# State-space decay without the causal mask product: Relu per head, one Exp over eight heads

## The reference, cut to what matters

```python
a_cs = jnp.cumsum(dt * A, axis=2)                      # A = -exp(a_log), so a_cs falls along time
seg = a_cs[:, :, :, None] - a_cs[:, :, None, :]        # a_l - a_s
decay = jnp.exp(jnp.where(causal, seg, -jnp.inf))      # 0 where s > l
cb = jnp.einsum('bclgn,bcsgn->bclsg', Cc, Bc)
y_diag = jnp.einsum('bclsg,bclsgr,bcsgrp->bclgrp', cb, decay, x)
states = ...                                           # carried from chunk to chunk
y = (y_diag + y_off) + d_skip * xh
```

## Time and profile before

| what | value |
|---|---|
| median of 3 runs | 1325.18 us (1324.61 to 1326.75) |
| span of the profiled execution, first to last instruction | 1311.2 us |
| median less span | 14.0 us |
| PE busy | 1269.9 us, 97% of the span |
| DVE busy | 640.5 us, 49% |
| ACT busy | 384.1 us, 29% |
| POOL busy | 725.5 us, 55% |
| mean granted PE clock | 0.996 |

### The profile page before, as it was taken

The page is one execution under the profiler, slowest core; times in us unless marked ns, Lnnn a source line. Parts: engine busy times, 40 slices in busy tenths (PEclk is TensorE's granted clock), DMA queues, the critical chain, the costliest instruction groups (busy, mean ns, idle before and its releaser), DMA issues.

```text
span 1311.2 us, 19028 instructions
## 1 busy us (share of the span) xinstructions
PE 1269.9 (97%) x7452; PEld 919.5 (70%) x7452; DVE 640.5 (49%) x1030; ACT 384.1 (29%) x763; POOL 725.5 (55%) x750
## 2 busy tenths in 40 slices
PE   8999989999999999999999999999999899999997
PEld 7888768787788776888888887788878333333333
DVE  4252361448993584624865678843315432222225
ACT  5211272422332584112122654441004011111111
POOL 6677636576675401766774445666771565555430
PEclk9999999999999999999999999999999999999999
DMA  6623311433232200343321314632277599999965
GB/s 232 188 75 107 96 34 31 151 121 97 65 129 97 97 1 1 96 133 120 102 64 52 94 49 145 266 135 97 95 287 292 215 373 408 406 403 405 402 244 192
DMA packets 86557, 216.40 MB, mean 165 GB/s; under 512 B 24260, under 2 KB 33196, under 8 KB 72900
## 3 DMA queue, kind: packets, MB, share of 16 engines
q1 hardware_dynamic: 62844, 199.23, 41.3%
q0 software_dynamic: 14064, 8.45, 2.2%
q10 hardware_dynamic: 9560, 7.51, 1.8%
HBM read 252.85 MB, written 25.96 MB: 213 GB/s over the span
## 4 chain that ended last, share of the span: by engine, by line
PE 74%; DMA 10%; DVE 7%; ACT 3%; DVEq 2%; POOL 2%; issue 1%; SPq 1%; ACTq 0%; POOLq 0%
PE ps L184 18%; PE ps L185 17%; PE ps L186 17%; DMA w_gu<-w_up 9%; PE ps L1204 7%; PE ps L1219 3%; PE ps L872 2%; POOL w_lo L1283 1%; PE ps L993 1%; PE ps L1077 1%; PE ps L1001 1%; DVE pr L2166 1%; ACT pr L1465 1%; SPq L559 1%; PE ps L971 1%
## 5 line engine op out<-in xcount | busy, mean ns | idle before, releaser
L1280 POOL CAST w_hi<-stage 128x512 fp32r<-128x512 f32 (+1 forms) x280 | 176.8, 674 | 358.6 <-PE ps L186 348.8
L1283 POOL TENSOR_TENSOR w_lo<-stage,w_hi 128x512 fp32r<-128x512 f32 (+1 forms) x280 | 367.7, 1345 | 10.1
L184 PE MATMUL ps<-hi,w_hi 128*128 128x512 f32 (+1 forms) x608 | 236.8, 389 | 0.8 <-ACTq L1666 0.5
L186 PE MATMUL ps<-lo,w_hi 128*128 128x512 f32 (+1 forms) x608 | 235.0, 386 | 0.0
L185 PE MATMUL ps<-hi,w_lo 128*128 128x512 f32 (+1 forms) x608 | 235.0, 386 | 0.0
L184 PE MATMUL ps<-w_hi,hi 128*128 128x512 f32 (+1 forms) x488 | 176.1, 361 | 2.4 <-DVE xtok L2290 0.9
L186 PE MATMUL ps<-w_lo,hi 128*128 128x512 f32 (+1 forms) x488 | 174.7, 358 | 0.0
L185 PE MATMUL ps<-w_hi,lo 128*128 128x512 f32 (+1 forms) x488 | 174.7, 358 | 0.0
L1204 PE MATMUL ps<-w_gu,xT 128*64 128x512 f32 x736 | 164.7, 600 | 3.7 <-DMA w_gu<-w_up 3.3
L184 PEld LDWEIGHTS ps<-hi,w_hi 128*128 128x128 f32 x608 | 114.2, 188 | 27.4 <-issue 3.4
L186 PEld LDWEIGHTS ps<-lo,w_hi 128*128 128x128 f32 x608 | 114.2, 188 | 23.3
(11 more groups left out here) (487 smaller groups left out, 1787.6 us busy)
## 6 DMA issues: line engine op xcount, KB each, us to landing
stage<-w_in SPq DMA_DIRECT2D x84, 512.0 KB, 4.5
w_gu<-w_gate SPq DMA_DIRECT2D x32, 1024.0 KB, 13.4
w_gu<-w_up SPq DMA_DIRECT2D x32, 1024.0 KB, 16.0
w_dn<-w_down SPq DMA_DIRECT2D x32, 1024.0 KB, 11.9
stage<-w_out SPq DMA_DIRECT2D x16, 512.0 KB, 4.6
stage<-w_ssd_branch SPq DMA_DIRECT2D x16, 512.0 KB, 4.7
stage<-w_in SPq DMA_DIRECT2D x20, 256.0 KB, 3.1
stage<-w_attn_branch SPq DMA_DIRECT2D x8, 512.0 KB, 4.3
```

The source lines that it names most:

```text
L184: pe.matmul(out, x[0], w[0], start=first, stop=False)
L186: return pe.matmul(out, x[0], w[1], start=False, stop=last)
L1280: nc.gpsimd.tensor_copy(hi[:, b, k, 0:n], stage[:, b, k, 0:n])
L1283: last = nc.gpsimd.tensor_tensor(lo[:, b, k, 0:n], stage[:, b, k, 0:n], hi[:, b, k, 0:n].bitcast(F32), ALU.subtract)
```

## The change

The mask product on PE (L1055) goes away, with the two DVE instructions that made `mask_r` and `ident_r`. ACT computes `relu(a_s - a_l)` for each head from PSUM, and then one Exp with scale -1 over eight heads, in place in SBUF. Where s > l the Relu gives 0 and the Exp 1; the zero comes from `cb`, which already carries the triangle. `acs[:, 0]` now holds `a_s` itself and not its negative. PE waits for `m_ready` once for each eight heads, and not once for the chunk. The waits for the four banks in `spread` stay, but no matmul stands between them now.

```diff
             def spread(c, half):
                 s = turns.take(ALL)
                 for b in range(4):
                     turns.bank(b, turns.k)
-                    pe.matmul(ps[s][:, b, :].rearrange("p (h l) -> p h l", h=4), ident_r[:], bc(mask_r[:], 1, 4), start=True, stop=False)
                 for j in range(4):
                     for b in range(4):
...
-                                         acs_rows[rows, P * c:P * (c + 1)], start=False, stop=(j == 3))
+                                         acs_rows[rows, P * c:P * (c + 1)], start=True, stop=True)
...
             pe.wait_ge(acs_copied, 1)
-            pe.wait_ge(acs_ready, 1)
...
-                pe.wait_ge(m_ready, 4 * (c + 1))
                 pe.wait_ge(xd_ready, c + 1)
                 s = turns.take()
                 for h in range(32):
+                    if h % 8 == 0:
+                        pe.wait_ge(m_ready, 4 * c + h // 8 + 1)
...
-            A.activation(acs[:, 2], acs[:, 0], ACT.Exp, scale=-1.0)
+            A.activation(acs[:, 2], acs[:, 0], ACT.Exp)
...
-                        last = A.activation(decay[:, hh, :], ps[s][:, h // 4, P * (h % 4):P * (h % 4 + 1)], ACT.Exp,
-                                            bias=acs[:, 0, c, hh:hh + 1])
+                        last = A.activation(decay[:, hh, :], ps[s][:, h // 4, P * (h % 4):P * (h % 4 + 1)], ACT.Relu,
+                                            scale=-1.0, bias=acs[:, 0, c, hh:hh + 1])
                         if h % 8 == 7:
-                            last.then_inc(e_ready, 1)
                             A.drain().then_inc(turn_free[s], 1)
+                            some = decay[:, hh - 7:hh + 1, :]
+                            A.activation(some, some, ACT.Exp, scale=-1.0).then_inc(e_ready, 1)
...
-            V.tensor_scalar(acs[:, 0], sums[:, :, 0, :], -1.0, None, ALU.mult)
+            V.tensor_copy(acs[:, 0], sums[:, :, 0, :])
...
-            V.tensor_tensor(acs[:, 1], acs[:, 3], acs[:, 0], ALU.add)
-            V.wait_ge(mT_saved, 16)
-            V.tensor_scalar(mask_r[:], tri[:], -1.0, -NEG, ALU.add, ALU.mult)
-            V.tensor_copy(ident_r[:], ident[:])
+            V.tensor_tensor(acs[:, 1], acs[:, 3], acs[:, 0], ALU.subtract)
             V.drain().then_inc(acs_ready, 1)
```

More of the change, by code:

```diff
@@ L322, in program @@
         acs = at("acs", 116, [P, 4, TT, 32])
-        mask_r, ident_r = at("mask_r", 112, [P, P], F32R), at("ident_r", 112.5, [P, P], F32R)
         sgb = at("sgb", 72, [P, KC, S])
```

## The result

The kernel after takes 1334.74 us (median of 4 runs, 1333.57 to 1337.79), the kernel before on the same chip 1325.14 us. The ratio is 1.0076, with a 95% interval of 1.0064 to 1.0088. It is slower by 9.6 us (difference of the medians) or 10 us (by the ratio), where 7.8 were forecast. A later comparison (e10) gave 1.0077 (1.0063 to 1.0092).

The account below looks back on a forecast made before the run. The prediction took ACT followed by DVE to bound the SSD stage, not PE; longer ACT groups and unhidden table loads, less the mask's saving, delay the last z projection 7.8 us: 1325.2 + 7.8 = 1333.0 us, range 1327.5 to 1337.

Parts of the forecast that it names:

- S0 to S3: Starts of ACT's first decay activation in chunks 0 to 3 of the SSD stage; forecast 724.4, 749.6, 778.6, 809.5.
- Groups of eight: ACT's eight Relus plus one Exp: 3.25 us a group, DVE's last multiply at S + 13.1, or S + 14.5 in chunks 1 to 3.
- The table load: Exp's load falls unhidden between first eight Relus and first Exp in chunks 1 to 3, 1.4 us each; rival, stays hidden: chance 0.13.
- Its 2.66 us for a switch: The skill's price for a table switch, load plus drain; by it the forecast would be 3.8 us higher.
- My sum: Chunk-by-chunk sum of ACT and DVE times to the last z projection: 837.8 against 829.95, 7.8 us later.
- The delay passes on: After the last z projection no slack absorbs the delay, so all 7.8 us reach the end; no-change rival: chance 0.05.

Follow-up runs that it names:

- e10: The kernel after, unchanged, measured again on another chip; ratio to the kernel before 1.0077.
- e3: Kernel after plus a one-column Exp behind the Silu of chunks 0 to 2, loading the table in ACT's idle time; ratio to before 1.0045.
- e2: Kernel after with one Exp per head (scale 0, timing only) in place of Relu and Exp over eight heads, still without mask matmuls; ratio to before 0.9999.
- e5: Kernel after with DVE's skip term moved ahead of the first multiply and from_state ahead of the second; ratio to before 1.0006.
- e4: Kernel after with the mask matmuls back in spread, Relu and Exp over eight heads kept; ratio to before 1.0105.
- e6: Kernel after with DVE's skip term and from_state moved, the early table load, and chunk 3's unread xe left out; ratio to before 1.0000.
- e8: e6 with mask matmuls back in the second spread of every chunk, as filler; ratio to before 0.9994.
- e9: e8 with the filler mask matmuls in the second spread of chunks 1 to 3 only; ratio to before 0.9995.
- e1: The kernel before, unchanged, measured and profiled again; ratio to before 0.9995.

## Why the prediction came out as it did

The direction, the mechanism and most of the size were right. Point by point, in distances from the stage's first table load, since everything before it ran 0.6 us earlier in this profile:

- **S0 to S3.** Forecast 2.0, 27.2, 56.2 and 87.1 us after the load (724.4 to 809.5 less 722.43). Measured 1.9, 26.8, 56.1 and 87.9 (723.77, 748.61, 777.96 and 809.71 less 721.86).
- **Groups of eight.** Forecast 3.25 us apart, measured 3.23; last multiply at S + 13.1 in chunk 0 and S + 14.5 later, measured 13.06 and 14.4.
- **The table load.** It fell where forecast, 2.27 us after S1. It cost 1.28, and 1.30 to the next activation; the runs with and without it (after and e3) differ by 3.6 us of D and 4.1 us of time, near my 4.1. From the end of the last Relu to the start of the Exp it is 1.39 us in chunk 1, drain and load together, where I had taken 1.4. The Trainium skill's place for the load was right (ScalarE: Activation LUTs, section Table sets). Its 2.66 us for a switch (section What ACT_TABLE_LOAD costs) did not show. The time alone could not have told: 1334.7 lies between my 1333.0 and the 1336.8 by its figure. (Its surplus over my 1.4 is 1.26 us a switch and not 1.28; the 3.8 us for three stand.)
- **The parts add up in D.** Mask gone 2.4 us less (e2), Exps over eight heads 7.2 more (e3 less e2), table loads 3.6 more (after less e3): 8.4 in all, which is 115.9 - 107.5. My sum gave 7.8.
- **The cause is ACT's time in series with DVE's.** The same ACT work costs little once DVE does the skip term and from_state before its multiplies: 1.9 us of D (e5 less e2), and nothing against before in the time (1.0006, interval over 1).
- **The delay passes on.** From D to E it grew by 1.3 us more (131.5 us after, 130.2 before), and E came 9.7 us later, which is the 10 us of the ratio.

The term that was mis-sized is the last: I passed on 7.8 us and reckoned with PE at full clock behind the new waits. PE waited 3.9 us, then ran at half clock, 8 matmuls where 14 fit, and lost 1.3 us there that nothing hid. The other profiles bear this out. The four with half clock at the start of the last z projection (after, e3, e10, e4) need 131.5, 131.7, 131.9 and 132.3 us from D to E; the eight without need 130.2 to 130.5. The half-clock stretches in chunks 1 and 3 cost the kernel after nothing that I can find, since DVE was the later one there.

The rest of the miss, 0.6 us of D, is a balance. S0 came 0.1 us early, chunk 0 was 0.35 us shorter than in my sum, chunk 1 0.35 longer and chunk 2 0.85 longer (31.75 us from S2 to S3 and not 30.9), the end 0.2 shorter. In chunk 2, L2286 began 8.9 us after the last multiply and S3 came 8.5 us after that, where I had 8.5 and 7.9. That the total came so close owes something to these terms of both signs.

I had also read the 14.0 us between span and median as if it lay around the span. It did not matter, because only a difference was added to the median, but comparing the two spans would have given twice the true effect.

Not tried: two or three Exps a chunk of other sizes, and another order of spreads and tokens on PE that would fill the wait before the second spread with useful work.

## What to carry to other kernels

Work moved from the busiest engine to an idle one is free only if nothing waits in line behind it: ask what follows the idle engine's last instruction, and add both. Here ACT was idle for 70% of the span, yet each group's extra microsecond came straight through because DVE had up to 6 us of unrelated work queued behind its last multiply; moving that work ahead of the wait gave back 9 us. Splitting a function in two can also bring a table load out of idle time, and a one-column activation of the right kind puts it back.

## What the runs showed of the hardware that was not expected

- The granted clock of PE fell to half, 1.2 GHz, after waits of a few microseconds in the stage: once behind the bank waits of chunk 3 in e2, twice in e6, three times in the kernel after.
- It does not follow from the length of the wait. In the kernel after PE waited 2.8 us before the second spread of chunk 2 and the clock stayed up; in e10, the same kernel, it fell behind the same 2.8 us. It also fell in e10 in chunk 0 (from about 722.5 us on) behind a wait of 1.4 us, where in the first profile it stayed up.
- Mask matmuls in part of the same waits (e8, e9) go with a clock that stays up there. One profile of each shows no more than that, since two profiles of one kernel differ in this; but the mean granted clock was 0.994 in all eleven timed executions of e8 and 0.990 to 0.994 in those of e6. For e9, 0.989 to 0.994, it was no steadier than for e6. Matmuls that compute nothing needed were not a pure loss: e9 with them has a D 2.0 us shorter than e6 without.
- Executions of one kernel on one chip differ in granted clock and time together: of the twenty of before beside e1 to e4, the seven at 0.993 took 2.0 us more in the mean than the nine at 0.996. That is as much as the stage gained in e2.
- The expert phase of one and the same kernel took 351.1 us in one profiled execution and 360.8 in another, with the stage before it the same to 0.1 us.
